# Order of the first loads and place of the modulation columns in a gMLP and attention layer

## The reference

```python
c_act = silu(c)
mod = c_act @ w_ada + b_ada                      # (B, 3D)
shift, scale, gate = split(mod, 3)
h = rms_norm(x, norm_w) * (1 + scale) + shift
proj = h @ w_in                                  # (B, S, 3584)
u_a, v_a, z_a, q_b, k_b, v_b, z_b = split(proj)  # 512 columns each
a_out = gmlp_spatial_gating(u_a, v_a, ...) * silu(z_a)
b_out = diff_attention(q, k, v_b, ...) * silu(z_b)
out = concat([a_out, b_out]) @ w_out
x = x + gate * out
```

## Time and profile before

| | us |
|---|---|
| median of 3 runs | 527.22 (526.07 to 529.1) |
| the profiled execution | 524.75 |
| its span on the slowest core (core 0) | 523.7 |
| the spans of the 8 cores | 518.9 to 523.7 |

### The profile page before, as it was taken

How to read it: one execution, slowest core, us unless ns; L and a number is a source line. 1 busy time by engine, 2 the same in 40 slices (tenths; PEclk the granted TensorE clock), 3 DMA queues, 4 the chain that set the end, 5 groups by cost and what they waited for, 6 DMA issues and landing times.

```text
span 523.7 us, 9735 instructions; the slowest of 8 cores (518.9 to 523.7 us)
## 1 busy us (share of the span) xinstructions
PE 443.3 (85%) x3104; PEld 213.6 (41%) x3104; DVE 334.4 (64%) x761; ACT 299.6 (57%) x402; POOL 85.0 (16%) x118
## 2 busy tenths in 40 slices
PE   0036697999999999999979999989997999999395
PEld 0002243444444443443326554444554555555242
DVE  1236845664765478888872676788658857868732
ACT  1056477446543247677777666666777778777100
POOL 1112500003760000000001111122222222122100
PEclk9998989999999999999988999999999999999979
DMA  8998989237433200050021212116822032011113
GB/s 200 269 304 233 253 295 132 65 58 164 102 139 103 81 1 2 1 76 6 1 80 41 63 61 77 46 42 206 279 83 82 27 98 80 13 70 41 41 69 133
DMA packets 15605, 53.90 MB, mean 103 GB/s; under 512 B 2242, under 2 KB 2626, under 8 KB 14660
## 3 DMA queue, kind: packets, MB, share of 16 engines
q1 hardware_dynamic: 13924, 45.36, 26.8%
q0 software_dynamic: 1152, 7.50, 9.1%
q10 hardware_dynamic: 480, 0.41, 0.3%
HBM read 50.29 MB, written 8.39 MB: 112 GB/s over the span
## 4 chain that ended last, share of the span: by engine, by line
PE 62%; DMA 10%; DVE 8%; ACT 7%; issue 6%; POOL 4%; SPq 0%; DVEq 0%; ACTq 0%; POOLq 0%
PE psum L648 14%; PE psum L470 13%; PE psum L1045 9%; PE psum L923 8%; DMA sb_WO<-w_adaT 5%; PE psum L893 5%; PE psum L1011 4%; ACT sb_cs L906 4%; DMA sb_kT<-xT 4%; POOL sb_cs L911 4%; PE psum L682 2%; DVE sb_F L980 2%; PE psum L669 1%; DVE sb_F L939 1%; PE psum L671 1%
## 5 line engine op out<-in xcount | busy, mean ns | idle before, releaser
L906 ACT ACTIVATE sb_cs<-psum,sb_small 128x1024 bf16<-128x1024 f32 x144 | 151.0, 1114 | 58.6 <-PE psum L893 58.6
L923 PE MATMUL psum<-sb_vB,sb_cs 128*128 128x129 bf16 x1088 | 88.2, 223 | 9.6 <-POOL sb_cs L911 6.1
L923 PEld LDWEIGHTS psum<-sb_vB,sb_cs 128*128 128x128 bf16 x1088 | 63.3, 99 | 39.8 <-issue 39.3
L911 POOL TENSOR_TENSOR sb_cs<-sb_cs,sb_constb 128x256 bf16<-128x256 bf16 x64 | 44.3, 695 | 216.4 <-ACT sb_cs L906 211.9
L470 PE MATMUL psum<-sb_W,sb_hT 128*128 128x512 bf16 x256 | 62.3, 404 | 15.5 <-ACT sb_hT L466 12.6
L893 PE MATMUL psum<-sb_qT,sb_kT 64*128 64x256 bf16 (+1 forms) x576 | 56.4, 272 | 6.5 <-ACT sb_cs L906 2.9
L648 PE MATMUL psum<-sb_hT,sb_W 128*128 128x512 bf16 x256 | 60.2, 378 | 0.0
L357 DVE SCALAR_TENSOR_TENSOR sb_F<-sb_WO,sb_F 128x1024 f32<-128x1024 f32 x24 | 30.2, 1258 | 30.5 <-DMA sb_WO<-w_adaT 22.0
L470 PEld LDWEIGHTS psum<-sb_W,sb_hT 128*128 128x128 bf16 x256 | 25.8, 102 | 51.5 <-issue 26.1
L436 PE MATMUL psum<-sb_vnA,sb_constb 128*128 128x512 bf16 x32 | 11.0, 471 | 32.5 <-ACT sb_vnA L429 32.5
L939 DVE COPY sb_F<-psum 128x258 f32<-128x258 f32 x64 | 24.2, 420 | 20.4 <-PE psum L923 20.3
(11 more groups left out here) (113 smaller groups left out, 543.2 us busy)
## 6 DMA issues: line engine op xcount, KB each, us to landing
sb_WO<-w_adaT SPq DMA_DIRECT2D x24, 512.0 KB, 7.6
sb_W<-w_in POOLq DMA_DIRECT2D x5, 1024.0 KB, 10.5
sb_W<-x SPq DMA_DIRECT2D x8, 512.0 KB, 4.9
sb_cs<-w_out SPq DMA_DIRECT2D x8, 512.0 KB, 3.5
sb_hT<-x SPq DMA_DIRECT2D x8, 512.0 KB, 12.2
out<-sb_hT SPq DMA_DIRECT2D x8, 512.0 KB, 2.8
out<-sb_W SPq DMA_DIRECT2D x6, 512.0 KB, 3.2
sb_qT<-xT SPq DMA_DIRECT2D x4, 512.0 KB, 22.7
```

Of the source, the lines that this page charges most:

```text
L906: act(lambda E: E.activation(out=et, in_=psum[:, X:X + 2, :], func=AF.Exp, bias=negM, scale=0.125), reads=[pb[X], pb[Y], b_lam], writes=[b ...
L911: pool(lambda E, em=em: E.tensor_tensor(out=em, in0=em, in1=tri_b.unsqueeze(1).broadcast_to([128, 2, 128]), op=ALU.mult), reads=[b_e[ei], ...
L923: pe(lambda E, u=u, j=j, c=c, i=i: E.matmul(psum[:, j, 256 * c:256 * c + 129], lhsT=et[:, c, QB * u + 128 * j:QB * u + 128 * (j + 1)], rhs ...
```

## The change

At the top, SyncE's queue now gets x block 0 first, then `c`, four modulation tiles, and all of x block 1; before, it got `c`, four tiles and x block 0, and x block 1 in two halves between the matvecs. The load of w_VB waits until tile 0 has landed. The load of w_ZB, before issued inside the first round of the loop, now stands behind the loop and waits until tile 11 has landed (`ada_dma[11]`). Silu of `c` moves behind the squares of block 0. `mod_kc` now consists of two operations on VectorE. The list of the start is reordered: block 0's first matmul steps stand ahead of most of the multiplications and of block 1's statistics, and a multiplication of block 1 stands ahead of each later pair of matvecs instead of behind it.

```diff
+    P.dma("pool", constb[:, :], cb_d, b_constb, writes=[b_constb])
+    load_xT(0)
     P.dma("sp", c_bc, c_d.rearrange("a n -> (a n)").partition_broadcast(128), b_F[0], writes=b_c)
-    P.dma("pool", constb[:, :], cb_d, b_constb, writes=[b_constb])
...
-    for j in ADA[0:4]:
-        load_ada(j, (0, 1, 2, 3))
-    load_xT(0)
-    load_w(0, G_VB)
+    ada_dma = [load_ada(j, (0, 1, 2, 3)) for j in ADA[0:4]]
+    load_w(0, G_VB, extra=[ada_dma[0]])
+    load_xT(1)
...
-    act(lambda E: E.activation(out=c_bc, in_=c_bc, func=AF.Silu), reads=b_c, writes=b_c)
...
-            load_ada(ADA[n + 4], (0, 1, 2, 3))
+            ada_dma.append(load_ada(ADA[n + 4], (0, 1, 2, 3)))
 
     def mod_kc(kc):
-        pool(lambda E: E.tensor_tensor(out=shift[:, kc:kc + 1], in0=modraw[:, kc:kc + 1], in1=bada[:, kc:kc + 1], op=ALU.add),
-             reads=[b_small, b_raw_[kc]], writes=[b_mod[kc]])
-        pool(lambda E: E.tensor_tensor(out=gvec[:, kc:kc + 1], in0=modraw[:, 8 + kc:9 + kc], in1=bada1[:, kc:kc + 1], op=ALU.add),
-             reads=[b_bada1, b_raw_[8 + kc]], writes=[b_mod[kc]])
-        pool(lambda E: E.tensor_tensor(out=gvec[:, kc:kc + 1], in0=gvec[:, kc:kc + 1], in1=normw[:, kc:kc + 1], op=ALU.mult),
-             reads=[b_small, b_mod[kc]], writes=[b_mod[kc]])
+        dve(lambda E: E.tensor_tensor(out=shift[:, kc:kc + 1], in0=modraw[:, kc:kc + 1], in1=bada[:, kc:kc + 1], op=ALU.add),
+            reads=[b_small, b_raw_[kc]], writes=[b_mod[kc]])
+        dve(lambda E: E.scalar_tensor_tensor(out=gvec[:, kc:kc + 1], in0=modraw[:, 8 + kc:9 + kc], scalar=bada1[:, kc:kc + 1],
+                                             in1=normw[:, kc:kc + 1], op0=ALU.add, op1=ALU.mult),
+            reads=[b_bada1, b_small, b_raw_[8 + kc]], writes=[b_mod[kc]])
...
-    phaseA(0)
+    for q in range(4):
+        phaseSq(0, q)
+        phaseMM(0, q)
+    act(lambda E: E.activation(out=c_bc, in_=c_bc, func=AF.Silu), reads=b_c, writes=b_c)
+    phaseLn(0)
     mv(0)
     mv(1)
-    load_xT(1, (0, 1))
+    mod_kc(0)
+    phaseM(0, 0)
+    start_mm(0, 0)
     mv(2)
     mv(3)
-    load_xT(1, (2, 3))
+    mod_kc(1)
+    start_mm(0, 1)
+    for q in range(1, 4):
+        phaseM(0, q)
+    for q in range(4):
+        phaseSq(1, q)
+        phaseMM(1, q)
+    phaseLn(1)
     mv(4)
     mv(5)
-    for kc in range(3):
-        mod_kc(kc)
-    for q in range(4):
-        phaseM(0, q)
-    for kc in range(2):
-        start_mm(0, kc)
-    phaseA(1)
+    mod_kc(2)
     start_mm(0, 2)
     for i in range(5):
         kc = 3 + i
+        if i < 4:
+            phaseM(1, i)
         mv(2 * kc)
         mv(2 * kc + 1)
         mod_kc(kc)
-        if i < 4:
-            phaseM(1, i)
         start_mm(0, kc)
         for k1 in ((0, 1), (2, 3), (4, 5), (6,), (7,))[i]:
             start_mm(1, k1)
-        if i == 0:
-            load_w(1, G_ZB)
         if i == 4:
             for tt in range(4):
                 vb_evac(tt, tt)
+    load_w(1, G_ZB, extra=[ada_dma[11]])
     load_xT(2)
     load_xT(3)
```

## The result

The changed kernel takes 531.5 us (median; 529.6 at best) where the kernel before, timed beside it, takes 528.5: a ratio of **1.0055, 95% interval 1.0030 to 1.0081**, some 2.9 us slower. The forecast was 527.6 on a median of 527.2, so +0.4 us; the time lies 0.3 us above the range. The profiled execution took 529.66 us.

The account below looks back on a forecast made before the run. DMA was taken to bound the kernel up to 65 us, with TensorE waiting for modulation, then TensorE. Terms gave +0.4 us at the statistics matmul; 524.75 + 0.4 = 525.15, or 527.6 us on the median's scale; range 523.2 to 531.2.

Parts of the forecast that it names:

- The prediction's sum: Start of the kernel: tile 15 at 65.1, first matmul 67.8, then 70.3, 79.0, statistics matmul 79.35 against 78.95, +0.4 us.
- the last step: TensorE's last 8 modulation matmuls, ahead of forty z-tile matmuls: 1.6 us (upper clock) to 3.4 (lower), 2.5 taken.
- The bound, and the shift reaching the end whole: Up to 65 us DMA limits and TensorE waits for modulation; a shift there should reach the end almost whole.
- Early start worth nothing: First projection matmul, at 39.56 before, comes some 8 us earlier but gains no time, since all hangs on tile 15.
- w_ZB and the last two tiles: w_ZB's load, waiting for tile 11, shares DMA time with tiles 14 and 15: +1.1 us, bounds -0.1 and +2.0.
- the signs: What the new profile would show, such as first projection matmul at 29 to 33, block 1's first multiplication at 43 to 46.
- The 1.7 us of lost DMA time: DMA engine time lost in 40 to 48 us comes back, and is lost again where VectorE frees a slot late.
- VectorE's pace: VectorE paces the modulation tiles at 4.1 us a pair against 3.3 of DMA; matvec 15 at 62.4 if data never late.
- Columns: Modulation columns behind matvec 15, two VectorE operations (0.5 us) replacing the GpSimd path (0.8): -0.3 us, bounds 0 and -0.5.
- The clock: TensorE's lower clock level during part of the forty z-tile matmuls, after its longer wait: 0 to 1.7 us, 0.4 taken.
- The slower rival: All of w_ZB ahead of tiles 14 and 15, and a cold TensorE: +3.9 us, 531.1 us; chance 0.23.
- The faster rival: Tiles 14 and 15 get ahead of w_ZB, VectorE's pace limits, matvec 15 at 62.4: -3.5 us, 523.7 us; chance 0.21.

## Why the prediction was wrong, point by point

The prediction's sum gave 79.35 for the statistics matmul; on the slowest core it is 82.51, 3.2 us later. **Two terms of the sum failed, both too small:** tile 15, 65.1 in the sum and a matvec at 66.98, is 1.9 us of it, and the last step with the z tiles at the lower clock, 11.55 summed and 12.83 measured, is 1.3. What lies between them, 2.7 us from matvec 15 to the first matmul, came out as summed.

- **The bound, and the shift reaching the end whole:** right. The span moves with the statistics matmul (371.4 to 375.2 us from the first z_A matmul to the end, as means, in every kernel here).
- **Early start worth nothing:** right, but it came at half the size. The first projection matmul is at 34.6 as a mean, 4 us earlier than before where some 8 was said, and later than the 29 to 33 of the prediction; no time comes with it.
- **w_ZB and the last two tiles, "+1.1 us, bounds -0.1 and +2.0":** the mechanism right, the term too small; measured are +2.3 to +3.4 against the two profiles of before. w_ZB was issued at 52.22 (52.0 forecast) and its first packets came at about 54.3 (54.4). DMA queues of the changed kernel in 54.3 to 64 us (packets, MB, share), the same core:

```profile
q0 software_dynamic: 130, 1.05, 80.3%
q1 hardware_dynamic: 112, 0.45, 18.3%
```

  130 GpSimd packets took 80.3% of 9.7 us on 16 engines, 0.96 us each, and a packet of SyncE's 0.25; the sum had 0.87 and 0.19 at the dear end, and took the middle between that and the 0.66 of the lone load. With 0.87 the working gave 66.0. With 0.96 and 0.25, for the 144 packets of w_ZB and the 256 of tiles 14 and 15, it gives 12.6 us and 66.9; tile 15 landed at 66.8. The queues also passed about one packet each in turn, 130 to 112. The Trainium skill, "DMA: Bandwidth & Descriptors", section "Queues, rings and completion order", says that an engine goes round the queues that have work and switches at packet boundaries; by that rule a dear packet on one queue holds each cheap one on the other for its whole length, and the trace agrees from 58 us on (87 packets to 91), less in the first 3.7 us (43 to 21).
- **That 52.2 fits 52.0 is luck.** Two errors cancel. Matvec 4 began at 38.46 where 41.7 was forecast, and the first multiplication of block 1 at 42.16 where it was 44.7 (43 to 46 in the signs), so tile 11 was asked for at 45.9 and not at 48.5. It then took 5.7 us to land and not 3.5, and w_ZB's issue came 0.6 us behind that. Tiles 14 and 15 were likewise asked for 2.7 us earlier than forecast, at 52.6 and 53.98, and gained nothing by it.
- **The 1.7 us of lost DMA time "come back, and are lost again":** wrong. The reckoning had no net change; measured are 3.1 us lost in 36 to 56 us (share 0.846 of 20 us) against 0.4 and 0.2 in the two profiles of before, so some 2.7 us of transfers more are left over behind that stretch. No term of the sum held this, since the sum starts at w_ZB's first packet. It shows in what was left: all of w_ZB and of tiles 14 and 15 was still to come at 54 us, where with eight slots tile 15 had been asked for at about 48.8. The runs with six and eight slots, which close the hole, bring matvec 15 from 66.7 to 63.7 and 62.5. The prediction had let each tile be asked for as its slot comes free, and had not asked what the DMA engines do until then; tiles 11 to 13 took 4.3 to 5.7 us to land.
- **VectorE's pace:** the size right. Pairs of 4.0 us (50.21 to 54.23) where 4.1 was reckoned; that it would set the tiles' time in the end was refuted by the run without multiplications.
- **Columns, -0.3 us:** right. From the last matvec's start to ScalarE it is 1.74 us (66.98 to 68.72) where it was 2.05. As a mean over the cores the path was shortened by more, 2.6 and 3.5 to 1.7, since GpSimd's tails go. That hides part of the late tile in the time.
- **The clock, "0 to 1.7, 0.4 taken", and 2.5 for the last step:** too small. From the first matmul to the statistics matmul are 12.83 us (69.68 to 82.51), where 11.55 were summed. That is +1.3 us, and the run with zero matmuls gives back 0.9 by the traces and 1.9 by the ratios. The prediction's 3.25 us for eight matmuls "at the lower" level is read from a row in a stretch with a granted clock of 1.00, so it is no price of the lower level.
- **The slower rival:** its result is what happened: 66.4 forecast for tile 15, 69.1 for the first matmul, 82.85 for the statistics matmul, 531.1 us; measured 66.98, 69.68, 82.51 and 531.5. In part that is luck, for its 66.4 follows from none of its own times: asked for at 55.3 and 56.7, with the 11.5 us of the slowest landing, tiles 14 and 15 would be there at 66.8 and 68.2. And its condition was wrong. It was to need w_ZB's first packets before tile 14 is asked for, and tile 11 at 53 or later. Tile 14 was asked for at 52.64, 1.7 us before the first of those packets, tile 15 at 53.98, and tile 11 was there by 52.2. What fits the trace, though no run separates it, is the order of issue: w_ZB had been issued at 52.22, 0.4 us ahead of tile 14, and its packets took 2.1 us to appear. In 53.5 to 54.3 us SyncE's queue moved 21 packets, 0.04 MB: tiles 12 and 13 were through but for stragglers, and tile 14's packets had hardly begun, so they met w_ZB's from the start.
- **The faster rival** (matvec 15 at 62.4, 523.7 us): the eight-slot kernel comes to the same numbers, 62.5 and 522.7, but by slots and not by GpSimd's stretching. The issue of w_ZB lasted 0.59 us and its first packet came 2.1 us after it, beside a VectorE busy for 3.78 us of 52 to 56. The rule of the Trainium skill, "SBUF — State Buffer", section "SBUF: two separate sides", would have spread its packets out if VectorE's operations ran in a two-port mode; that they did no run here shows, and neither does any show such a spread.

## What to carry to other kernels

Where transfers are paced by free slots, count the slots against the landing time and look for holes in the DMA share before adding anything to the queues; here two more slots turned +0.55% into -0.4% and four into -0.7%, with a change whose order had looked like a loss. A transfer on an in-order queue is held by whatever stands ahead of it: moving small operations off that queue moved a 1 MB load's issue forward by 34 to 38 us (on core 7 from 45.38 to 7.70), and in four of these experiments it was released by something else than intended. A tile whose load is asked for just ahead of a dearer load's first packet is caught by it all the same. And a long wait for the last tile is paid twice, as a wait and in TensorE's clock behind it: two of the runs here took back the whole loss without bringing the tile any sooner.

## What the runs showed of the hardware that was not expected

- A packet of w_ZB (8 KB) costs 0.96 us of an engine and one of SyncE's (4 KB) about 0.25 (18.3% over 112) while both queues have work, and they go about one for one; so beside 1.05 MB on GpSimd's queue a 512 KB tile took 12.8 us to land, where 512 KB on a quiet queue took 3.5.
- From a load's issue to its first packet on GpSimd's queue passed 2.1 us (52.22 to about 54.3).
- One-column operations on GpSimd took 0.19 us or, beside VectorE without a pause, 0.64 to 1.26 and at times 3.57 us.
- TensorE's granted clock fell to the lower level in its wait of 8.4 us and stayed there past the first matmuls of the burst (0.50 in 68 to 72 us, 0.79 in 72 to 76). Extra matmuls inside that wait kept it up, for a gain of 0.9 us by the traces and 1.9 by ratios whose intervals overlap. Where they stood with real matmuls before and behind them and no wait, they lost 2.7 us in one kernel, and 1.2 in another, with an interval that takes in none.
